# A new opening, an even deal of w_ada's chunks over the first quarters of w_in, and both attention maps copied by ScalarE

## The reference

```python
mod = silu(c) @ w_ada + b_ada                 # w_ada: 2048 x 12288
shift_a, scale_a, gate_a, shift_f, scale_f, gate_f = split(mod, 6)
h = rms_norm(x, g_attn_pre) * (1 + scale_a) + shift_a
proj = h @ w_in                               # w_in: 2048 x 5456
diff_out = rms_norm((softmax(q1 k1) - lam * softmax(q2 k2)) v, g_diff_sub) * 0.2   # 8 heads
dsa_out  = top-64 sparse attention, 8 heads, one shared k and v, keys picked by an indexer of 16 heads
x = x + gate_a * rms_norm(concat(diff_out, dsa_out) @ w_o, g_attn_post)
h = rms_norm(x, g_ffn_pre) * (1 + scale_f) + shift_f
x = x + gate_f * rms_norm((silu(h @ w_gate) * (h @ w_up)) @ w_down, g_ffn_post)
# second block: norm, w_in_2 (latents, gates), 16-head latent attention, a gated convolution of
# width 3, w_o_mla_2, w_o_conv_2, w_out_2, norm, residual
```

## Time and profile before

| | |
|---|---|
| median of 3 runs | 2403.71 us (2403.37 to 2404.49) |
| profiled execution | 2403.83 us, span 2402.5 us, mean granted clock 0.982 |
| TensorE busy | 2288.5 us, 95% |
| VectorE busy | 1400.4 us, 58% |
| ScalarE busy | 1065.3 us, 44% |
| DMA | 505.69 MB, mean 210 GB/s |

### The profile page before, as it was taken

One profiled execution on the slowest core, in us unless ns is written; L12 is line 12 of the kernel. 1 busy time (PEld: TensorE's weight loads), 2 busy tenths in 40 slices (PEclk: granted clock), 3 DMA queues, 4 the chain that ended last, 5 costly groups with the idle time before them and its releaser, 6 DMA issues.

```text
span 2402.5 us, 26312 instructions
## 1 busy us (share of the span) xinstructions
PE 2288.5 (95%) x10768; PEld 1858.3 (77%) x10768; DVE 1400.4 (58%) x1903; ACT 1065.3 (44%) x1471; POOL 0.7 (0%) x5
## 2 busy tenths in 40 slices
PE   4899989889999999999998999999999999999998
PEld 2676767777888888888887878888888888888886
DVE  1459999795775464554456554545544554554554
ACT  2333544444444444434444555555444444444443
POOL 0000000000000000000000000000000000000000
PEclk7999999998999999999999999999999999999999
DMA  7888678593786675556553744444565555555553
GB/s 295 332 321 297 228 263 305 196 357 123 272 281 219 202 253 190 180 194 195 187 193 118 237 149 154 149 154 153 193 193 193 186 184 193 191 191 195 180 188 140
DMA packets 255455, 505.69 MB, mean 210 GB/s; under 512 B 9077, under 2 KB 19662, under 8 KB 254182
## 3 DMA queue, kind: packets, MB, share of 16 engines
q1 hardware_dynamic: 255334, 504.00, 62.2%
HBM read 499.77 MB, written 4.19 MB: 210 GB/s over the span
## 4 chain that ended last, share of the span: by engine, by line
PE 86%; DVE 7%; ACT 3%; DMA 2%; issue 1%; SPq 0%; DVEq 0%; ACTq 0%
PE bank L595 27%; PE bank L597 26%; PE bank L596 26%; DVE wlo L1674 2%; PE bank L611 2%; DMA raw<-in_w_in_dram 2%; DVE acc L1655 1%; PE bank L679 1%; ACT whi L1062 1%; DMA raw<-in_w_ada_dram 1%; PE bank L549 1%; PE bank L619 1%; DVE x L1726 0%; PE bank L702 0%; PE bank L531 0%
## 5 line engine op out<-in xcount | busy, mean ns | idle before, releaser
L1674 DVE TENSOR_TENSOR wlo<-raw,whi 128x1024 fp32r<-128x1024 f32 (+2 forms) x760 | 912.8, 1205 | 871.9 <-ACT whi L1062 870.2
L1062 ACT ACTIVATE whi<-raw 128x1024 fp32r<-128x1024 f32 (+2 forms) x760 | 789.9, 1044 | 1037.9 <-PE bank L597 917.5
L595 PE MATMUL bank<-whi,Ahi 128*128 128x512 f32 (+2 forms) x2304 | 910.8, 395 | 33.6 <-DVE wlo L1674 22.2
L596 PE MATMUL bank<-wlo,Ahi 128*128 128x512 f32 (+2 forms) x2304 | 896.6, 389 | 0.0
L597 PE MATMUL bank<-whi,Alo 128*128 128x512 f32 (+2 forms) x2304 | 896.4, 389 | 0.0
L595 PEld LDWEIGHTS bank<-whi,Ahi 128*128 128x128 f32 x2304 | 437.3, 190 | 132.9 <-DVE wlo L1674 31.9
L597 PEld LDWEIGHTS bank<-whi,Alo 128*128 128x128 f32 x2304 | 437.2, 190 | 90.2
L596 PEld LDWEIGHTS bank<-wlo,Ahi 128*128 128x128 f32 x2304 | 437.9, 190 | 83.4
L1655 DVE SCALAR_TENSOR_TENSOR acc<-raw,cs,acc 128x512 f32<-128x512 f32 x224 | 157.2, 745 | 0.1
L595 PE MATMUL bank<-whi,Fhi 128*128 128x512 f32 x352 | 137.6, 391 | 0.0
L597 PE MATMUL bank<-whi,Flo 128*128 128x512 f32 x352 | 137.1, 389 | 0.0
(11 more groups left out here) (291 smaller groups left out, 1344.3 us busy)
## 6 DMA issues: line engine op xcount, KB each, us to landing
raw<-in_w_in_dram SPq DMA_DIRECT2D x156, 1024.0 KB, 5.0
raw<-in_w_ada_dram SPq DMA_DIRECT2D x96, 1024.0 KB, 6.8
raw<-in_w_gate_dram SPq DMA_DIRECT2D x44, 1024.0 KB, 5.1
raw<-in_w_up_dram SPq DMA_DIRECT2D x44, 1024.0 KB, 5.1
raw<-in_w_down_dram SPq DMA_DIRECT2D x44, 1024.0 KB, 5.0
raw<-in_w_o_dram SPq DMA_DIRECT2D x16, 1024.0 KB, 6.7
raw<-in_w_o_mla_dram SPq DMA_DIRECT2D x16, 1024.0 KB, 4.9
raw<-in_w_o_conv_dram SPq DMA_DIRECT2D x16, 1024.0 KB, 4.9
```

What stands on the lines that cost most here:

```text
L595: pe.matmul(o, a_hi, w_hi, start=beg, stop=False)
L596: pe.matmul(o, a_hi, w_lo, start=False, stop=False)
L1062: act.activation(m.whi[:, i % NHL, :, 0:n], m.raw[:, c % NRAW, 2 * h:2 * h + 2, 0:n], ACT.Copy).then_inc(m.s_hi, 1)
L1674: dve.tensor_tensor(m.wlo[:, i % NHL, :, 0:n], m.raw[:, c % NRAW, 2 * h:2 * h + 2, 0:n], m.whi[:, i % NHL, :, 0:n].bitcast(F32), ALU.subtr ...
```

## The change

Five things change together.

1. The gain vectors, c and b_ada are handed over already in columns, the positions and the lambdas in one array each, and x also turned (features on partitions, `x_turned`). The start loads columns, chunk 0, constants, chunk 1, the turned x in two halves, chunk 2, b_ada's columns, chunks 3 and 4; positions and lambdas follow chunk 8. x in its own layout comes later in four pieces of 0.5 MiB, each behind a chunk of w_in's second late column group (`at_x`), into the room that the turned x had.
2. 1/rms is found over partitions: ScalarE squares the turned x, VectorE reduces over the 8 blocks of each half (a strided read), TensorE sums over partitions with a matrix of ones after its fifth chunk, ScalarE takes the root and VectorE the reciprocal over 256 elements.
3. h's quarters are made without TensorE: VectorE multiplies the turned x by scale and 1/rms as soon as the scale is known (`first_scale`), ScalarE adds the shift and rounds, VectorE adds the shift and subtracts (`first_shift`).
4. w_ada's chunks are dealt otherwise (DEAL_PE for TensorE's, DEAL_VECTOR for VectorE's), four of VectorE's are moved ahead into quarters 1 and 2, and half of TensorE's between two w_in chunks are multiplied between the two units of the first. W_IN_SHARE falls to 24, and w_o has 14.
5. ScalarE copies both maps.

```diff
+DEAL_PE = ((3, 3, 2, 2, 1), (2, 2, 1, 1, 1), (2, 2, 2, 0, 0), (0, 0, 0, 0, 0))
+DEAL_VECTOR = ((0, 0, 0, 0, 0), (0, 0, 0, 1, 1), (0, 0, 0, 1, 1), (1, 1, 1, 1, 2))
+W_IN_SHARE = 24
...
+            for some, n in ((first, DEAL_PE[q][i]), (rest, DEAL_VECTOR[q][i])):
+                plan += some[:n]
+                del some[:n]
...
@@ tensor_program
+                c = LIN[i][0]
+                some = ada_beside(c) // 2
+                if h == 0:
+                    ada_products(c + 1, some)
+                else:
+                    ada_products(c + 1 + some, ada_beside(c) - some)
...
+    def beside(idx, j):
+
+        if (idx, j) == (1, 0):
+            need.wait_ge(m.s_const, 16)
+            k.use(4)
+            for h in range(2):
+                need.wait_ge(m.s_red, h + 1)
+                ins = pe.matmul(m.bank[4][:, 0:S], m.ones, m.red[:, h, :], start=(h == 0), stop=(h == 1))
+            ins.then_inc(m.filled[4], 1)
+        if (idx, j) == (1, 2):
+            ada_columns(0)
...
-    ada_products(0)
-    first_operand(0)
+    ada_products(0, 8, beside)
+    ada_columns(1)
     for q, cg in WIN_ITEMS[:3 * len(W_IN_FIRST)]:
         first_part(q, cg)
+        if cg == W_IN_FIRST[2]:
+            ada_columns(2 * q + 2)
         if cg == W_IN_FIRST[3]:
-            first_operand(q + 1)
+            ada_columns(2 * q + 3)
...
@@ scalar_program
+    need.wait_ge(m.s_cols, 16)
     act.activation(m.sig[:, :], m.cols[:, R_C:R_C + 16], ACT.Sigmoid).then_inc(m.s_sig, 1)
...
+    for h, o in enumerate((m.sq[:, :, :], m.tmpA[:, :, :, :].rearrange("p a k t -> p (a k) t"))):
+        need.wait_ge(m.s_xT[h], 16)
+        act.activation(o, m.xT[:, 8 * h:8 * h + 8, :], ACT.Square).then_inc(m.s_sq, 1)
+    warm_sqrt()
+    need.wait_ge(m.filled[4], k.use(4))
+    act.activation(m.rms[:, :], m.bank[4][:, 0:S], ACT.Sqrt, bias=m.eps[:, :], scale=1.0 / D).then_inc(m.freed[4], 1)
...
     def first_operand(q):
...
+        for j in range(2):
+            need.wait_ge(m.s_t, 2 * q + j + 1)
+            need.wait_ge(m.freed[7], shift_at)
+            for kk in (2 * j, 2 * j + 1):
+                kb = 4 * q + kk
+                ins = act.activation(m.Ahi[:, kb, :], m.tmpA[:, q % 2, kk, :], ACT.Identity, bias=m.modT[:, kb:kb + 1])
...
-            copy_out(ln.ET[:, 0:384], b0, ex[0], m.bank[b0][:, 0:384])
+            for mm, b in enumerate(ln.bank[0:nm]):
+                copy_out(ln.ET[:, 384 * mm:384 * mm + 384], b, ex[mm], m.bank[b][:, 0:384])
...
-        copy_out(ln.ET[:, 0:384], 4, ex[0], m.bank[4][:, 0:384])
+        for mm in range(2):
+            copy_out(ln.ET[:, 384 * mm:384 * mm + 384], 4 + mm, ex[mm], m.bank[4 + mm][:, 0:384])
...
@@ vector_program
+        need.wait_ge(m.s_sq, k.up(m.s_sq))
+        dve.tensor_reduce(m.red[:, h, :], i.rearrange("p k t -> p t k"), AX_X, ALU.add).then_inc(m.s_red, 1)
+    need.wait_ge(m.freed[4], k.use(4))
+    rstd_at = v.up(dve.reciprocal(m.rstdT[:, :], m.rms[:, :]))
...
+        for kk in range(4):
+            kb = 4 * q + kk
+            ins = dve.scalar_tensor_tensor(out=m.tmpA[:, q % 2, kk, :], in0=m.xT[:, kb, :], scalar=m.gs[:, kb:kb + 1],
+                                           in1=m.rstdT[:, :], op0=ALU.mult, op1=ALU.mult)
...
+    def first_shift(q):
+
+        k.use(7)
+        mod(ADA_ON_PE[2 * q + 1], 7, k.use(7))
+        if q == 0:
+            k.split_to(UNIT_AT[LIN[1]])
...
+            for kk in (2 * j, 2 * j + 1):
+                kb = 4 * q + kk
+                ins = dve.scalar_tensor_tensor(out=m.Alo[:, kb, :], in0=m.tmpA[:, q % 2, kk, :],
+                                               scalar=m.modT[:, kb:kb + 1], in1=m.Ahi[:, kb, :].bitcast(F32),
+                                               op0=ALU.add, op1=ALU.subtract)
...
-                need.wait_ge(m.filled[b1], ex[1])
-                dve.tensor_copy(ln.ET[:, 384:768], m.bank[b1][:, 0:384]).then_inc(m.freed[b1], 1)
...
-        need.wait_ge(m.filled[5], ex[1])
-        dve.tensor_copy(ln.ET[:, 384:768], m.bank[5][:, 0:384]).then_inc(m.freed[5], 1)
...
@@ sync_program
+    sp.dma_start(m.cols[:, :], A["columns"]).then_inc(m.s_cols, 16)
+    load_chunk(0)
     sp.dma_start(m.const[:, :], A["consts"]).then_inc(m.s_const, 16)
...
+    load_chunk(1)
+    for h in range(2):
+        sp.dma_start(m.xT[:, 8 * h:8 * h + 8, :], A["x_turned"][:, 8 * h:8 * h + 8, :]).then_inc(m.s_xT[h], 16)
+    load_chunk(2)
+    sp.dma_start(m.bT[:, :], A["bias_columns"]).then_inc(m.s_bT, 16)
+    for c in range(3, NRAW):
...
+    at_x = [chunk_ahead(unit_after("w_in", 4 * q, 512 * W_IN_ORDER[1]) - 1) for q in range(4)]
...
+        if c == LIN[0][0]:
+            sp.dma_start(m.pos[:, :], A["positions_both"]).then_inc(m.s_pos, 16)
+            sp.dma_start(m.lraw[:, :, :].rearrange("p a d -> p (a d)"),
+                         A["lambdas"].broadcast_to([P, 256])).then_inc(m.s_lamin, 16)
+        if c in at_x:
+            tb, h = divmod(at_x.index(c), 2)
+            need.wait_ge(m.s_shlo, 8)
+            cols = slice(1024 * h, 1024 * h + 1024)
+            sp.dma_start(x[:, tb, cols], A["x"][0, tb * P:tb * P + P, cols]).then_inc(m.s_x, 16)
```

More of the change, by code:

```diff
@@ L59, in lin @@
         plan.append(("lin", w, k0, c0, n))
[L61 to L64, removed]
+    first = [("ada", g, j) for g in ADA_ON_PE for j in range(4)]
+    rest = [("ada", g, j) for g in range(8, 20) for j in range(4)]
+    plan += first[:8]
+    del first[:8]
     for q in range(4):
@@ L67, in chunk_plan @@
             lin("w_in", 4 * q, *win_cols(cg))
-            n = (BETWEEN if q < 3 else BETWEEN_LAST)[i]
-            plan += rest[:n]
-            del rest[:n]
+            for some, n in ((first, DEAL_PE[q][i]), (rest, DEAL_VECTOR[q][i])):
+                plan += some[:n]
+                del some[:n]
+    assert not first
     late = len(rest)
@@ L162, with ada_beside @@
 UNIT_AT = {u: i for i, u in enumerate(UNITS)}
+def ada_beside(c):
+    n = 0
+    while c + n + 1 < len(PLAN) and PLAN[c + n + 1][0] == "ada" and c + n + 1 not in ADA_NO:
+        n += 1
+    return n
 def unit_after(w, k0, c0):
@@ L536, in ada_take, with ada_products @@
             ins.then_inc(m.filled[b], 1)
-    def ada_products(c):
-        while c < len(PLAN) and PLAN[c][0] == "ada" and c not in ADA_NO:
+    def ada_products(c, n, beside=None):
+        for c in range(c, c + n):
             _, g, j = PLAN[c]
@@ L551, in ada_products @@
             ins.then_inc(m.s_prod if j < 3 else m.filled[b], 1)
-            c += 1
+            if beside:
+                beside(ADA_ON_PE.index(g), j)
     def ada_columns(idx):
@@ L1779, in shifted, with first_scale @@
             ins.then_inc(m.freed[b], 1)
[L1780 to L1794, removed]
+            ks = slice(4 * q + 2 * j, 4 * q + 2 * j + 2)
+            need.wait_ge(m.s_shhi, base + 2 * q + j + 1)
+            dve.tensor_tensor(m.Alo[:, ks, :], tmp[:, q % 2, 2 * j:2 * j + 2, :], m.Ahi[:, ks, :].bitcast(F32),
+                              ALU.subtract).then_inc(m.s_shlo, 1)
+    def first_scale(q):
+        k.use(6)
+        mod(ADA_ON_PE[2 * q], 6, k.use(6))
+        released(mod_at[4 + q])
         ks = slice(4 * q, 4 * q + 4)
@@ L2550, in constants, with laid_out, rows @@
     return c
[L2553 to L2556 removed]
+_INS = ["x", "w_ada", "b_ada", "g_attn_post", "g_ffn_post", "w_in", "w_o", "w_gate", "w_up", "w_down", "w_in_2",
+        "w_q_b_2", "w_kv_b_2", "w_o_mla_2", "w_o_conv_2", "w_out_2", "post_norm_g_2"]
+def laid_out(inputs):
+    def rows(name):
+        return np.asarray(inputs[name]).reshape(-1, P)
+    columns = ("c", "g_attn_pre", "g_ffn_pre", "pre_norm_g_2", "q_a_norm_g_2", "kv_a_norm_g_2", "conv_w_2", "g_diff_sub")
+    return {
+        "columns": np.concatenate([rows(n) for n in columns]).T,
+        "bias_columns": rows("b_ada").T,
+        "positions_both": np.concatenate([rows(n) for n in ("positions", "positions_2")]).T,
+        "lambdas": np.concatenate([np.asarray(inputs[n]) for n in ("lambda_q1", "lambda_k1", "lambda_q2", "lambda_k2")],
+                                  axis=1),
+        "x_turned": np.asarray(inputs["x"])[0].T.reshape(KD, P, S).transpose(1, 0, 2),
+        "consts": constants(),
+    }
 def kernel(**inputs):
```

173 lines of the change are left out of this document (66 added, 107 removed).

## The result

The changed kernel takes 2378.34 us (median of four, 2375.13 to 2379.99) against 2403.72; the ratio is 0.9892 with a 95% interval of 0.9875 to 0.9909. The profiled execution took 2377.72 us, its span is 2376.4. The forecast was 2369.4, -34.4; it is -25 to -26. So the direction and most of the mechanism held, and some nine microseconds are missing.

The account below looks back on a forecast made before the run. TensorE's matrix work was taken to hold 86% of the chain, leaving its idle time to win, with a transfer-bound early stage. Terms -24.5 + 1 - 3.5 - 7.4 = -34.4 took 2403.83 to 2369.4 us; range 2359 to 2383.

Parts of the forecast that it names:

- part 1: Opening: the eighth w_ada chunk lands at 30.3 us instead of 39.9, -9.6; first w_in matmul at 36.6.
- part 2: Quarters 0 to 2, new deal: DMA binds, quarter 2's fourth w_in chunk lands at 137.5; -24.5 us including the opening's -9.6.
- half the pauses: Rival for the quarters: the ring, not the deal, makes the loads pause; +9 to 12 us, some 2380; chance 0.14.
- part 3: Quarter 2's fourth w_in chunk to quarter 3's end: VectorE gets two more chunks; +1 us, from -2.8 to +5.6.
- part 4: Rest of w_in and w_o: VectorE has fewer chunks and map copies; -3.5 us, between 0 and -7.2.
- the sparse maps: Sparse attention: half of its map copies go from VectorE to ScalarE; a gain of 0.5 us.
- part 5: Second block: both maps copied on ScalarE, TensorE's wait shrinks by 1.0 us seven times; -6.9 us.
- The clock rival: Pauses keep TensorE at 1.2 GHz to quarter 2's end; +57 us there, some 2451 in total; chance 0.02.

Follow-up runs that it names:

- the lone chunk: Changed kernel, but a w_ada chunk standing alone behind a w_in chunk is multiplied between its two units instead of after both: 2375.40 us, 0.9887.
- all three edits: Changed kernel with angle tables and lambda made in the opening, lone w_ada chunks between units, VectorE's four chunks put back: 2370.27 us, 0.9870.

## Why the prediction was right in sign and nine microseconds too good

**The opening (part 1)** was right step by step: -12.6 at the first matmul for -12.2. The two reductions took 3.67 us each where the contiguous row gave 3.3, so the price was nearly right. It was right in part by luck: the row of 0.42 us for 256 contiguous elements holds a fixed part. The same reduction over 128 elements took 0.284 us and over 256 0.415, so each further element costs 1.02 ns; 2048 at that rate would be some 2.2 us (an estimate from these two rows), where the 2048 elements 1 KB apart took 1.79 ns each. The Trainium skill's penalty for each new 16-byte line (SBUF — State Buffer, "Door 1: The DMA port swizzle") may be in that difference. The trace doesn't single it out, since the two also differ in source (SBUF, PSUM) and in the number of sums (256, one). The reciprocal took 1.75 us, inside the slack.

**The quarters (part 2)** is the step that failed: -24.5 predicted at chunk 13, -14.8 measured. The claim was that the DMA binds in each quarter, with 3 us left for friction. The miss at chunk 13, 9.7 us, is past the worst case of the forecast for this part (half the pauses, 9.3). By its own signs it was wrong too: it asked for no pause below 300 GB/s between 40 and 130 us, and the DMA moved 268, 172 and 256 in the three stretches of 5 us from 75 on and 266 from 110 to 115; quarter 3 ended at 201 instead of 187. In quarter 0 the DMA did bind up to 75 us (share 1.05 from 36 to 76). Three things stood against the claim from there.
- The tables' chain. I priced each edit that goes and named its cover, but did not ask what the turning of x had itself been covering. The run with the tables in the opening got 5.0 us back in quarter 0, and the moved loads cost it 2.1 ahead of it.
- The places held by lone w_ada chunks: 4.1 us into quarter 2. The prediction says "half of a group of w_ada is consumed after the first unit"; half of one is none.
- TensorE's own work. Quarter 1 takes 35.8 us from chunk 5 to chunk 10, foreseen 33.8, with no wait in it, and the tables, the lone chunk and VectorE's chunks leave it at 35.7 to 36. The likely reason: the row at 63.68 gives three products in a row, 0.93 each; set apart, a unit and one product take 3.95 us (91.12 to 95.07) where a unit within a chunk takes 2.72, so 1.23 each. I multiplied seven dispersed products by the price of bundled ones; 7 x 0.3 = 2.1 is what is missing. The run with all products after both units bears on it: it joins two pairs of them in quarter 1, which takes 35.5 us with a wait of 0.4 in it, so 0.7 less of TensorE's work. That fits, though no run bundles all seven.

With the first two undone and VectorE's chunks back, chunk 13 starts at 141.5, with a first matmul 2.6 us later than the changed kernel's; the prediction (landing 137.5, split 2.4) had 139.9. So the arithmetic of bytes was sound, and the claim about what binds was not: with those pauses gone it is TensorE that is full from 76 us on. The rival "half the pauses stay" (2380) was the nearest to the total, 2378.3, though it named only the ring, which is one of the three.

**From there to quarter 3's end (part 3):** +1 predicted, +4.4 measured (lead 14.8 to 10.4), within the bounds of -2.8 and +5.6. VectorE was busy 36.62 of 36.90 us. I had hidden the first of its two chunks in a wait for a transfer; putting all four back removes the loss (the lead goes from 18.9 to 20.1).

**The rest of w_in and w_o (part 4):** predicted -3.5 and -0.5 for the sparse maps; measured -8.4 (10.4 to 18.8), near the lower bound. Of these 1.7 come at the one chunk after the norm, in which some traces have the long matmuls of the lower clock and others not: the granted clock there is 0.80 in the kernel before and 1.00 in the changed kernel, but 0.78 with the tables alone and 0.76 with all products after both units, whose leads fall by 0.3. Each kernel has one trace, and both levels occur with and without the change, so I take it as luck of a run. The other 6.7 are the same 6.7 that putting the four chunks back gives away up to chunk 48. So parts 3 and 4 are one term: VectorE's chunks are paid for in full wherever VectorE is full, and I had halved the price. The total profits from it: part 3 was 3.4 us worse than forecast and part 4 was 4.4 better, 1.7 of them chance. The 0.5 for the sparse maps has no support in the run of the maps alone.

**The second block (part 5):** -6.9 predicted, -6.9 measured (lead 18.8 at chunk 214, 25.7 at 251), -6.8 by the maps alone. Each step came as told.

**The clock rival** did not occur: the granted clock was 0.96 from 36 to 76 us, 0.97 from there to 127 and 0.95 from there to 160.

| term | predicted | measured |
|---|---|---|
| opening, to the first matmul | -12.2 | -12.6 |
| from there to chunk 13 | -12.3 | -2.2 |
| to chunk 20 | +1 | +4.4 |
| to the second block | -4 | -8.4 (1.7 of it chance) |
| second block | -6.9 | -6.9 |
| sum | -34.4 | -25.7 |

## What to carry to other kernels

When work is taken away, ask not only what hid it but what it hid: a chain of short steps over two engines that was free beside it may become the next wait. In a ring of buffers the price of a step that is moved is when it gives its place back, not how long it takes; and a count that is halved by whole numbers leaves the lone one where it was. Compare two traces by the start of the same unit of work in both: gains that are only moved (here VectorE's chunks, 6.7 us one way and back) are plain there and hidden in any sum of busy times.

## What was not expected of the hardware

- RECIPROCAL over 256 elements on VectorE took 1.75 us, 6.8 ns an element; a reduction over elements 1 KB apart took 1.8 ns an element read, against 1.02 for each further element of a contiguous row (0.284 us for 128, 0.415 for 256).
- With two loads of 128 short runs each (16 B and 1 KB) sent ahead of chunk 1, every w_ada chunk of the opening from the second on was used later, by 2.0 to 2.1 us with the tables alone and by up to 2.7 with all three edits.
- A group of 8 short matmuls set between two runs of w_in matmuls costs 1.23 us, three groups together 2.78.
- After a wait of 2.25 us the next seven matmuls started 0.43 us apart instead of 0.23 (76.85 to 80.00), 1.6 us more, with a granted clock of 0.67 from 75 to 80 us; after others of like length (46.66, 2.19) they did not.
